# A two-layer attention kernel: the grid attention in tiles of eight rows by sixteen columns, two gate buffers, keys written in two steps, and bias tables laid out whole

## The reference, cut to what matters

```python
def window_gqa(q, k, v, sink, rel_bias):          # layer 0, 8 heads
    rel = kpos[None, :] - qpos[:, None]           # 128 queries, 384 keys around them
    band = jnp.abs(rel) <= WINDOW                 # 128
    bias = rel_bias[t5_bucket(rel)]
    s = q @ k * scale + bias ; s = where(valid, s, -inf) ; softmax with a sink

def neighborhood_attn(q, k, v, rpb):              # layer 1, 16 heads of 64
    cs = jnp.clip(col - 8, 0, 64 - 16)            # a query sees 16 columns ...
    rs = jnp.clip(r - 4, 0, 16 - 8)               # ... of 8 rows
    bias = rpb[h, key_row - r + 7, key_col - col + 15]
    s = q @ k * scale + bias ; outside of the window -inf ; p = softmax(s) ; p @ v
...
    y = concat([yc, ym]) * silu(gate) ; x = x + y @ w_out
```

## Time and profile before

| | |
|---|---|
| time, median of 3 runs | 2720.52 us (2718.27 to 2722.08) |
| profiled execution, time | 2720.37 us |
| profiled execution, span | 2718.6 us |
| PE busy | 2513.0 us, 92% of the span |
| PEld busy | 2102.3 us, 77% |
| DVE busy | 1403.0 us, 52% |
| ACT busy | 1266.6 us, 47% |
| POOL busy | 852.1 us, 31% |

### The profile page before, as it was taken

How to read it: one execution, slowest core, us unless ns; L and a number is a source line. 1 busy time by engine, 2 the same in 40 slices (tenths; PEclk the granted TensorE clock), 3 DMA queues, 4 the chain that set the end, 5 groups by cost and what they waited for, 6 DMA issues and landing times.

```text
span 2718.6 us, 37117 instructions
## 1 busy us (share of the span) xinstructions
PE 2513.0 (92%) x12984; PEld 2102.3 (77%) x12984; DVE 1403.0 (52%) x2795; ACT 1266.6 (47%) x2900; POOL 852.1 (31%) x1053
## 2 busy tenths in 40 slices
PE   4898889999998999988999999898989999999999
PEld 4687777777887778877877878786767888888877
DVE  6424476766776433345566555668585512321331
ACT  5333455565676433445555555554454412322331
POOL 2233211111125552211211112356675522322222
PEclk8798999999999999999999999999999999999999
DMA  4421210111224332111222111332222311111112
GB/s 155 139 66 51 58 28 16 35 29 36 53 77 132 90 101 70 55 53 49 57 57 53 46 46 53 100 111 71 78 74 82 93 51 47 47 49 49 51 41 91
DMA packets 306675, 179.49 MB, mean 66 GB/s; under 512 B 63771, under 2 KB 289307, under 8 KB 305980
## 3 DMA queue, kind: packets, MB, share of 16 engines
q1 hardware_dynamic: 306492, 177.12, 22.5%
HBM read 157.15 MB, written 19.92 MB: 65 GB/s over the span
## 4 chain that ended last, share of the span: by engine, by line
PE 69%; DVE 14%; ACT 7%; issue 7%; POOL 3%; DMA 1%; SPq 0%; ACTq 0%; DVEq 0%; POOLq 0%
PE PS L1352 18%; PE PS L1354 18%; PE PS L1353 18%; PE PS L1478 4%; PE PS L1449 4%; DVE QKV L1779 2%; PE PS L1436 2%; PE PS L1437 2%; POOL WS L2149 2%; ACT PY L1574 1%; ACT PT L1574 1%; DVE PY L1900 1%; ACT QKV L1574 1%; DVE YB L1945 1%; PE PS L1489 1%
## 5 line engine op out<-in xcount | busy, mean ns | idle before, releaser
L2149 POOL TENSOR_TENSOR WS<-WR,WS 128x256 fp32r<-128x256 f32 (+1 forms) x946 | 731.7, 790 | 1729.8 <-ACT WS L1574 1728.9
L1352 PE MATMUL PS<-HT,WS 128*128 128x512 f32 x2080 | 841.3, 404 | 31.9 <-POOL WS L2149 13.2
L1354 PE MATMUL PS<-HT,WS 128*128 128x512 f32 x2080 | 819.5, 394 | 0.0
L1353 PE MATMUL PS<-HT,WS 128*128 128x512 f32 x2080 | 819.1, 394 | 0.0
L1574 ACT ACTIVATE WS<-WR 128x256 fp32r<-128x256 f32 x988 | 369.5, 407 | 381.2 <-PE PS L1354 343.5
L1352 PEld LDWEIGHTS PS<-HT,WS 128*128 128x128 f32 x2080 | 396.3, 191 | 130.9 <-issue 31.0
L1354 PEld LDWEIGHTS PS<-HT,WS 128*128 128x128 f32 x2080 | 395.2, 190 | 86.0
L1353 PEld LDWEIGHTS PS<-HT,WS 128*128 128x128 f32 x2080 | 396.1, 190 | 74.7
L1779 DVE TENSOR_TENSOR PT<-PS,PT 128x512 fp32r<-128x512 f32 (+2 forms) x384 | 243.5, 638 | 169.4 <-ACT PT L1574 167.7
L1574 ACT ACTIVATE PT<-PS 128x512 fp32r<-128x512 f32 (+2 forms) x384 | 211.7, 552 | 254.2 <-PE PS L1449 253.9
L1478 PE MATMUL PS<-PT,QKV 128*128 128x256 f32 (+1 forms) x1376 | 239.5, 296 | 26.3 <-DVE YB L1945 22.5
(11 more groups left out here) (157 smaller groups left out, 2774.8 us busy)
## 6 DMA issues: line engine op xcount, KB each, us to landing
WR<-in_ffn_in SPq DMA_DIRECT2D x120, 256.0 KB, 2.9
WR<-in_w_in_odd SPq DMA_DIRECT2D x106, 256.0 KB, 3.0
WR<-in_w_in_even SPq DMA_DIRECT2D x100, 128.0 KB, 2.5
WR<-in_w_out_odd SPq DMA_DIRECT2D x48, 256.0 KB, 2.8
yd<-PY SPq DMA_DIRECT2D x44, 256.0 KB, 3.2
PY<-yd SPq DMA_DIRECT2D x36, 256.0 KB, 3.3
WR<-in_w_in_even SPq DMA_DIRECT2D x34, 256.0 KB, 2.9
WR<-in_w_mem SPq DMA_DIRECT2D x32, 256.0 KB, 2.8
```

What stands on the lines that cost most here:

```text
L1352: e.matmul(out, wh, rh, start=start, stop=False)
L1353: e.matmul(out, wh, rl, start=False, stop=False)
L1354: return e.matmul(out, wl, rh, start=False, stop=stop)
L2149: e.tensor_tensor(WS[:, i % NSPL, 1, 0:n], WR[:, u % NRAW, o:o + n], f32(WS[:, i % NSPL, 0, 0:n]), ALU.subtract).then_inc(s_wlop.sem, 1)
```

## The change

The grid chunks are tiled anew. A tile is eight rows by sixteen columns of queries; its keys are twelve rows by 32 columns, 384 in all, for every tile. A chunk has again eight tiles for each head and eight jobs, but no tile takes two banks: the grid chunks now run as the windowed ones of layer 0, both scores of a job side by side. Q is written reordered by tiles, K is read in place as twelve pieces of 32 columns, and V is laid out by four column windows into `FG` (three ACT copies a half) and transposed in four groups instead of two. The bias comes as complete tables, 48 loads of 128 by 768 floats, and the windowed one as four loads; nothing is made on the chip. `FG`, and a second gate buffer, lie in chunks 1 to 3 of X, which are kept in DRAM meanwhile ("x keep", "x back"). Both halves of the next chunk's gate are projected during a chunk. The two heads of a key half leave as two steps ("leave", "other head"). `reload` begins earlier and has more buffers.

```diff
-        HOT = EO[0:33, 2048:2560]
-        EDGE = [EO[:, 1536 * x:1536 * x + 896] for x in (0, 1)]
-        INNER = [EO[:, 1536 * x + 896:1536 * x + 1536] for x in (0, 1)]
+        BT = [EO[:, 768 * i:768 * i + 768] for i in range(4)]
+        SGB = [SG[:, :], X[:, 3, :]]
+        FG = [X[:, 1, :], X[:, 2, :]]
+        YG = PY[:, 2560:3584]
...
+        def other_head(h):
+            yield False
+            h.va, h.vd = s_ea.n, s_ed.n
+            s_ea.add(2)
+            s_ed.add(2)
+            h.end = (s_ed, s_ed.n)
+            put("other head", h)
+            ready[h.to[0]] = [h.end]
...
+                    if c.grid:
+                        for j, part, n in ((c.j, 1, 2 * pp + h - 1), (c.j + 1, 0, 2 * pp + h - 5)):
+                            if n in (0, 1) and 0 < j < 8:
+                                require(f"vc{j}")
+                                flip_grid(grid_v[f"vc{j}", n], part)
...
-                return Chunk(12 + i, 1, i, kind, j, slot, (j + 1) % 2, lambda t: (c_keys[t][0], 128 * c_keys[t][1]),
-                             (f"q1{i}", f"kc{j}", f"vc{j}"), (3, 640), True, "c", None)
+                return Chunk(12 + i, 1, i, kind, j, slot, (j + 1) % 2, lambda t: (t % 2, 384),
+                             (f"q1{i}", f"kc{j}", f"vc{j}"), (4, 384), False, "c", None)
...
+        def table_read(j, pp, h):
+
+            if pp != 1:
+                v = (0, 1, 1, 2)[pp]
+                table_end[table_at[j, v, h][0]] = s_mx.n
+                table_load()
...
-        put("hot load")
         put("mem keep", mem_end)
         put("tables")
-        put("window vectors")
...
+                            if c.grid:
+                                q = q_at(c.q_slot, h)[:, 512 * s.x + 128 * s.pp:512 * s.x + 128 * s.pp + 128]
+                                col = (0, 8, 24, 32)[s.pp]
+                                kh, kl = (k_at(c.kv_slot, h, part).rearrange("p (r c) -> p r c", c=64)[:, 4 * s.x:4 * s.x + 12, col:col + 32]
+                                          for part in (0, 1))
...
-                    e.tensor_tensor(e3, e3, CM[:, :].unsqueeze(1).to_broadcast([128, 14, 64]), ALU.add).then_inc(s_cb.sem, 1)
...
+                elif kind == "x keep":
+                    for nm in l1:
+                        w.wait_ge(s_nd, nm.nd[7])
+                    for c in (1, 2, 3):
+                        e.dma_start(d["xk"][c - 1, :, :], X[:, c, :]).then_inc(d_keep.sem, 16)
...
+                elif kind == "table load":
+                    j, v, h, i, mx = of
+                    for sig, value in l1[1].lo[4:]:
+                        w.wait_ge(sig, value)
+                    w.wait_ge(s_mx, mx)
+                    e.dma_start(BT[i], d["grid"][2 * j + h, v, :, :]).then_inc(d_bt[i].sem, 16)
```

More of the change, by code:

```diff
@@ L86, in __init__ @@
         self.wide, self.bias, self.sink = wide, bias, sink
-        self.mem = kind == "m"
+        self.mem, self.grid = kind == "m", kind == "c"
+        self.sg = 1 if self.grid and i % 2 == 0 else 0
         self.nh = 1 if self.mem else 2
@@ L611, in finish @@
         def finish(c, pp):
-            require(f"g{c.layer}{c.i}:{pp // 2}")
+            for n in (0, 1) if c.grid else (pp // 2,):
+                require(f"g{c.layer}{c.i}:{n}")
             f = Fin(c, pp, s_spread.add(), s_fin.n, s_yc.n, s_pv.n, c.rec[pp])
@@ L795, in chunk_loop @@
             marks.append(len(tasks))
-            for oc in range(8):
+            for oc in range(8) if layer == 0 else (0, 4, 5, 6, 7, 1, 2, 3):
                 first_out(oc)
@@ L812, in chunk_loop @@
                 if i == 11:
-                    last_chunk(att, marks[12], end, reload(layer))
+                    last_chunk(att, marks[12], end, reload(layer, mine, marks[12]))
                     break
@@ L1003, in start_chunk @@
         def start_chunk(c):
-            if c.kind == "c" and c.j == 0:
-                for x in (0, 1):
-                    bias_load(0, x)
-                    put("bias make", *bias_make.pop(0))
+            if c.layer == 1 and c.i == 0:
+                put("x keep")
+                d_keep.add(48)
+            if c.layer == 1 and c.i == 3:
+                for _ in range(4):
+                    table_load()
         mem_norm = Norm(lambda c: MX[:, c, :], MEM, SM, 0, B_O)
@@ L1389, in tensor_program @@
                         m.then_inc(s_mm.sem, 1)
-                        until[h.bank] = (s_ea, h.ea + 1) if h.kind in ("v", "rope") else (s_ed, h.ed + OPS[h.kind][1])
+                        until[h.bank] = h.end
                     elif h.last:
@@ L1457, in tensor_program @@
                     first, final = i == 0, i == len(job.banks) - 1
-                    for sig, value in ready[c.wants[2]]:
+                    for sig, value in ready[(c.wants[2], job.pp // 2) if c.grid else c.wants[2]]:
                         w.wait_ge(sig, value)
@@ L1811, in vector_program @@
                     a, b = 512 * h.n, 512 * h.n + 512
[L1812 removed]
+                    if h.kind in ("v", "vg", "rope"):
                         continue
@@ L2305, in build, with band_tables @@
         block.tensor(tensor_program)
+def band_tables(rel_bias):
+    f = np.float32
+    rel = np.arange(384)[None, :] - 128 - np.arange(128)[:, None]
+    n = np.abs(rel)
+    large = 8 + (np.log(np.maximum(n, 1).astype(f) / f(8)) / f(math.log(16)) * f(8)).astype(np.int32)
+    bucket = np.where(rel > 0, 16, 0) + np.where(n < 8, n, np.minimum(large, 15))
+    p, k = np.nonzero(n <= 128)
+    out = np.full((4, 128, 2, 384), NEG, rel_bias.dtype)
+    for h in range(8):
+        out[h % 4, p, h // 4, k] = rel_bias[bucket[p, k], h]
+    return out
 def shape_constants():
```

507 lines of the change are left out of this document (265 added, 242 removed).

## The result

| | before | after |
|---|---|---|
| median of 4 runs each, same chip | 2719.99 us (2718.27 to 2722.08) | 2588.22 us (2585.84 to 2592.72) |
| profiled execution, time / span | 2720.37 / 2718.6 us | 2589.86 / 2588.1 us |

The ratio is 0.9517, with an interval of 0.9501 to 0.9534: 131.8 us or 4.8% faster. Forecast were 120.4 us, 2600 with a range of 2575 to 2650. So the sign and the range held, and the gain was 11.4 us larger than forecast. It is larger in some places and smaller in another, so part of this closeness is luck: errors of 24 and of 12 us stand against each other. Of the times that the prediction stated, 2581 us (*more goes*) is nearer to the 2588 than 2600 is.

What follows compares the result with a forecast made beforehand. PE, busy for 92% of the span, was taken as the bound. 86.4 (grid chunks) + 20.7 (window vectors) + 4.4 (grid start) + 6 + 2.9 (last chunks) = 120.4 us off 2720.4, so 2600 us, range 2575 to 2650.

Steps and rivals of the forecast that it cites:

- more goes: Rival, chance 0.13: the B_X wait and all 8.4 us of last-chunk waits go too, 19 us more, 2581 us.
- The grid chunk: Layer 1's grid chunks, run like windowed ones: 68.0 us instead of 78.8, 8 x 10.8 = 86.4 us.
- the one wait that I expect to stay: Grid chunk: the spread still waits 2.1 us for bank B_X while DVE takes V out behind four key instructions.
- forecast of 6.3 us by instruction count: Grid chunk: fewer scores, transposes and value matmuls, less eight more V transposes, save 6.3 us a chunk or 50 us.
- only the instructions go: Rival, chance 0.17: the idle 4.5 us a grid chunk stay; 50 + 20.7 + 4.4 = 75 us go, 2645 us.
- Start of the grid stage: Mask additions on DVE, waiting for strips to land, hold PE at 1163 us; they go: 4.4 us.
- Window vectors: PE stretch between the memory's V transposes and the first projection goes whole: 20.7 us, ends 15 and 20.7.
- Last chunk of layer 0: The wait for a row maximum goes, with 18 and 30 matmuls where 6 and none stood: 2.9 us.
- Last grid chunk: Of 8.4 us of score waits for row maxima 6 go, beyond an ordinary chunk's 10.8; ends 0 and 8.4.
- Costed at nothing: Table loads, x keep and x back, and keys in two steps, at 0; upper end 5 us for layer 1's end loads.
- slower: Rival, chance 0.05: table loads on SP's queue delay weight loads, 48 x 3.0 = 144 us, 2744 us.
- strided keys cost: Rival, chance 0.05: grid score matmuls reading keys in twelve pieces take double, 45 us come back, 2645 us.

Runs made afterwards that it cites:

- e2: Changed kernel with one gate buffer, each chunk's gate projected in its own chunk ahead of the keys, Q last: 2629.45 us, ratio 0.9664.
- e8: Kernel before with grid tiles cut to 384 keys, scores still apart, bias still made on the chip, different output: 2641.62 us, ratio 0.9705.
- e9: Kernel before with two lines exchanged, so that K is projected before V in a grid chunk: 2698.08 us, ratio 0.9916.
- e1: Changed kernel with a grid job's scores issued one after the other again, 12 projection matmuls behind each: 2617.42 us, ratio 0.9609.
- e5: e2 with both gate buffers back and its order of projections kept: 2638.33 us, ratio 0.9693.
- e4: Kernel before with the windowed bias loaded as four finished tables and the window vectors stretch removed: 2698.77 us, ratio 0.9915.
- e6: Changed kernel with each of the 48 table loads followed by a second, DRAM to DRAM transfer of the same size: 2584.46 us, ratio 0.9496.
- e11: Changed kernel without the two buffers for y added to reload in layer 1: 2595.97 us, ratio 0.9531.
- e7: Changed kernel with the early stores of held-back results taken out of reload: 2589.63 us, ratio 0.9511.
- e3: Changed kernel with scores reading 384 neighbouring keys in one piece, so of other keys: 2586.85 us, ratio 0.9502.
- e10: Changed kernel with the keys of both heads leaving in one step again: 2585.72 us, ratio 0.9507.

## Why the prediction was right, and where it was off

**The grid chunk, 86.4 us forecast.** The method held: the sum of jobs from layer 0's windowed chunk gave 65.9 us, and the steady chunk takes 66.7. Wrong was the step "to it I add the one wait that I expect to stay", 2.1 us. The prediction had the order on DVE right (keys, then a V group), but took it that a spread would come close behind. It stands in another job, and e2 shows what the forecast wait looks like when it is there, e8 and e9 that it hangs on this position with either tile. The rival *more goes* had this wait vanish for another reason, less for DVE to do; e1, e2 and e8 speak against that reason, since DVE has nearly as little to do in each (39, 39 and 41 us, against 38) and the spread waits. Its number for these chunks was the better one all the same. A steady chunk gained 12.1 us instead of 10.8, 5.0 us more over chunks 6 to 9.

**Instructions or waits.** The forecast of 6.3 us by instruction count agrees with what comes out when each matmul is given the usual distance to the next start (71.9 us before, 65.4 after, so 6.5). The waits, open and half hidden, gave 5.6, not 4.5. One price was a little low: a transpose starts 0.109 us behind the one before, not 0.09, and a spread, with 64 columns of weights instead of 128, 0.054 us. Both multiply 128 columns, so that it is the weights loaded that set their distance, as the prediction read from the value matmuls. The rival *only the instructions go* would have been right with the order of e2: e2 and e5 took 2629 and 2638 us, near the 2645 of that rival.

**Start of the grid stage, 4.4 us forecast.** Of the terms that came out larger, this one was missed by the most. Chunks 3 to 5 gained 39.2 us for equal work where two chunks and the 4.4 made 26.0. The prediction read one wait there, and not the clock behind the waits. Windows of 4 us of the kernel before, each behind a wait of PE of 2.7, 4.4, 3.8 and 2.8 us:

```profile
1132.00:1136.00 4.00, 4.00 (x14) 3.18 (x13) 1.58 (x6) 1.86 (x7) 2.15 (x3) 0.57 0.04 7
1172.00:1176.00 4.00, 4.00 (x16) 3.21 (x15) 1.25 (x5) 1.12 (x3) 0.74 (x1) 0.82 0.00 0
...
1208.00:1212.00 4.00, 4.00 (x13) 3.25 (x13) 1.23 (x4) 1.53 (x4) 1.17 (x2) 0.62 0.23 62
1252.00:1256.00 4.00, 4.00 (x15) 3.39 (x14) 2.71 (x5) 1.84 (x5) 0.73 (x1) 0.58 0.39 90
```

The granted clock falls behind each of them. The means of chunks 3, 4 and 5 were 0.96, 0.94 and 0.97, which is 71.6 x 0.04 + 77.3 x 0.06 + 83.4 x 0.03 = 10.0 us of lost clock; after the change they are 1.00, 1.00 and 0.98, 1.4 us. So 8.6 us of clock come back. The waits themselves fall from 20.6 us (1100.9 to 1333.2) to 3.9 (1073.3 to 1271.8). With two chunks' instructions, 2 x 6.5, this makes 16.7 + 8.6 + 13.0 = 38.3 of the 39.2. So of the 13.2 us that the forecast was short here 8.6 are clock, a term that it put at nothing. That size isn't exact: e4 has the grid chunks of the kernel before and loses 6.2 us of clock there, with 229.7 us in all instead of 232.3. How much each edit has in it wasn't tried, except that e9 alone brings chunk 4 from 77.3 to 70.4.

**Window vectors, 20.7 us forecast.** Right, and e4 shows it alone. The 20.9 of the changed kernel are 19.7 at the first projection, since the transposes for V come 1.2 us later there (they wait 1.56 us for ACT, before 0.47), and 1.2 of clock behind it, which the prediction didn't have.

**Last chunk of layer 0, 2.9 us forecast.** It gained 3.4, but only in part for the reason given, so the hit is partly luck. The wait of 2.9 us is gone, but one for weights grew from 2.5 to 4.0; PE idles in this stretch for 12.9 us where it did for 14.3, and the lost clock (one minus the granted clock, summed) falls from 3.4 to 1.7 us. With the same order there, e6 takes 195.4 us for it and e11 198.8. The other 3.3 us of layer 0 can't be shown to be a gain of the change: PE idles as long (49.8 and 49.7 us), and only the clock differs, as it does between executions of one order.

**Last grid chunk, 16.8 us forecast (10.8 and 6).** Here the gain was mis-sized: 4.8 us. This is the term of the sum that failed: the 6 us of idle time, and the idle part of the 10.8, were to go. The 8.4 us of waits of scores in the earlier trace rows are gone, as forecast. In their place the projections of chunk 11 and behind it wait: 7.8 us for split weights where it was 2.7, 3.2 for y and 1.8 for weights on ACT where it was 0 and 0.5 (the 3.1 for X were there before). Over the whole row of the table PE idled for 21.4 us and now idles for 24.7, so the gain is the 8.1 us by which its busy time fell, less these 3.3. Chunk 11 itself went from 83.5 to 73.1 us, and the stretch behind it, with 30 matmuls more than before, from 138.5 to 144.1. The prediction counted the matmuls behind each job and never asked what feeds them: with the chunk shorter, the 48 weight tiles of the output product and the y to be reloaded come due earlier (DMA goes at 175 GB/s in that chunk, where it was 127 before; 83 in a steady one). That the cause lies in the feed is read from the waits; e7 excludes the stores, e11 leans towards the buffers, and the rest is open.

**Costed at nothing.** The table loads (e6), strided keys (e3) and the keys in two steps (e10) cost and give nothing measurable. The rivals *slower* and *strided keys cost* are out. In e10 the order of the grid stage is the same as in the changed kernel, so it prices the two steps for layer 0 alone. What the prediction did not name at all is the order of the projections that two gate buffers allow, which by e2 and e5 is worth 41 to 50 us.

## What to carry to other kernels

A job of the same shape elsewhere in the trace gave a chunk's time to within about 1% here (65.9 for 66.7 us); but for each shared PSUM bank, find which job its next user stands in before calling a wait retained or gone: an exchange of two lines was worth 23 us here. Read the granted clock behind each wait of PE as well as the wait, since in the kernel before the lost clock at the four windows above came to 1.7, 1.7, 3.0 and 3.4 us. Where a stage gets shorter, ask whether what is loaded for the next one arrives as much earlier.

## What was not expected of the hardware

A wait of PE of only 2.1 to 2.3 us can be followed by some 3.5 us at half the clock. In e5, between 1270 and 1510, each of the six such waits was, with matmuls of 512 columns 0.43 us apart instead of 0.23. In e2, in the same stretch, only one of seven such waits was. In the kernel before, the 2.1 us of the earlier trace rows left it at 1.00, and waits of 2.7 to 4.4 us were each followed by a window with a granted clock of 0.57 to 0.82. The length of the wait doesn't decide it: of e8's six waits of 2.84 us the ones at 1263.7 and 1403.2 left the clock at 1.00 and the other four did not, and in e1 a wait of 1.03 us was enough at 1372.0, followed by a window of 4 us at 0.57, while one as long at 1302.9 was not.

The steady grid chunks repeat within 0.2 us from one kernel to the next, but layer 0, with the same instructions and the same idle time, took from 847.5 us (e6) to 856.7 (e11), by the clock that was granted in it.
